# A two-layer encoder trunk with routed experts: the hot expert's extra part worked on fourth instead of seventh

## The reference

```python
def hierarchical_moe(h, w_rg, b_rg, w_re, b_re, w_gate, w_up, w_down):
    """Top-1 expert group, then top-2 SwiGLU experts inside that group."""
    ...
    for grp in range(MOE_GROUPS):
        hid = (jax.nn.silu(jnp.einsum('td,edf->tef', t, w_gate[grp]))
               * jnp.einsum('td,edf->tef', t, w_up[grp]))
        out = out + jnp.einsum('tef,efd->td', hid * gate[:, grp, :, None].astype(hid.dtype), w_down[grp])
    return out.reshape(b, s, d).astype(h.dtype)
```

## Time and profile before

| | us |
|---|---|
| median of 3 runs | 622.05 |
| lowest and highest | 620.03, 623.84 |
| profiled execution, its own time | 622.66 |
| its span in the trace | 620.9 |
| TensorE busy (matmul) | 545.1 (88%) |
| VectorE busy | 336.7 (54%) |
| ScalarE busy | 245.2 (39%) |
| GpSimd busy | 81.2 (13%) |

### The profile page before, as it was taken

The page is one execution under the profiler, slowest core; times in us unless marked ns, Lnnn a source line. Parts: engine busy times, 40 slices in busy tenths (PEclk is TensorE's granted clock), DMA queues, the critical chain, the costliest instruction groups (busy, mean ns, idle before and its releaser), DMA issues.

```text
span 620.9 us, 11990 instructions
## 1 busy us (share of the span) xinstructions
PE 545.1 (88%) x5109; PEld 451.7 (73%) x5109; DVE 336.7 (54%) x593; ACT 245.2 (39%) x457; POOL 81.2 (13%) x99
## 2 busy tenths in 40 slices
PE   2899986779979888884999999999999989788986
PEld 2899985679756466641999999899989856366642
DVE  2456759974562333447599655546646562433355
ACT  3453555254433133314545642443324533133221
POOL 6600242410100000001200290001110100000000
PEclk9999997969898999999899979999998898999999
DMA  8995400013989999999565252000021999999992
GB/s 310 276 344 167 170 2 1 1 68 125 398 341 413 410 406 409 409 410 374 170 204 186 66 194 69 2 3 4 2 69 66 407 335 392 409 409 409 409 409 112
DMA packets 55893, 145.24 MB, mean 234 GB/s; under 512 B 4260, under 2 KB 29040, under 8 KB 55712
## 3 DMA queue, kind: packets, MB, share of 16 engines
q1 hardware_dynamic: 54752, 142.47, 60.7%
q0 software_dynamic: 1088, 2.00, 1.5%
HBM read 143.40 MB, written 1.05 MB: 233 GB/s over the span
## 4 chain that ended last, share of the span: by engine, by line
PE 76%; DVE 13%; ACT 5%; issue 4%; DMA 2%; POOL 1%; SPq 0%; DVEq 0%; ACTq 0%
PE PS L1830 11%; PE PS L510 7%; PE PS L1791 7%; PE PS L511 7%; PE PS L512 6%; PE PS L1852 6%; PE PS L1866 3%; PE PS L546 3%; PE PS L547 3%; PE PS L548 3%; DVE WL L506 2%; PE PS L1867 2%; DVE X L1100 2%; PE PS L2126 2%; DMA RAW<-ev_w_in 2%
## 5 line engine op out<-in xcount | busy, mean ns | idle before, releaser
L506 DVE TENSOR_TENSOR WL<-RAW,WH 128x768 fp32r<-128x768 f32 (+2 forms) x96 | 82.8, 906 | 59.0 <-ACT WH L500 57.8
L510 PE MATMUL PS<-WH,HTH 128*128 128x384 f32 (+2 forms) x272 | 91.8, 338 | 3.1 <-DVE HTL L1100 1.4
L511 PE MATMUL PS<-WL,HTH 128*128 128x384 f32 (+2 forms) x272 | 90.3, 332 | 0.0
L512 PE MATMUL PS<-WH,HTL 128*128 128x384 f32 (+2 forms) x272 | 90.1, 331 | 0.0
L1100 DVE TENSOR_TENSOR X<-PS,X 128x512 f32<-128x512 f32 (+2 forms) x84 | 52.4, 662 | 62.6 <-PE PS L1867 49.0
L500 ACT ACTIVATE WH<-RAW 128x768 fp32r<-128x768 f32 (+2 forms) x96 | 70.7, 796 | 18.2 <-PE PS L512 10.4
L510 PEld LDWEIGHTS PS<-WH,HTH 128*128 128x128 f32 x272 | 53.1, 195 | 4.7 <-DVE HTL L1100 2.2
L511 PEld LDWEIGHTS PS<-WL,HTH 128*128 128x128 f32 x272 | 53.1, 195 | 0.0
L512 PEld LDWEIGHTS PS<-WH,HTL 128*128 128x128 f32 x272 | 52.8, 194 | 0.0
L546 PE MATMUL PS<-HTH,WH 128*128 128x256 f32 x160 | 46.6, 291 | 3.8 <-DVE HTL L1100 3.8
L547 PE MATMUL PS<-HTL,WH 128*128 128x256 f32 x160 | 46.1, 288 | 0.0
(11 more groups left out here) (344 smaller groups left out, 1051.1 us busy)
## 6 DMA issues: line engine op xcount, KB each, us to landing
RAW<-moe_w_gate SPq DMA_DIRECT2D x32, 512.0 KB, 11.3
RAW<-moe_w_up SPq DMA_DIRECT2D x32, 512.0 KB, 12.3
RAW<-moe_w_down SPq DMA_DIRECT2D x32, 512.0 KB, 13.9
XG<-moe_w_gate SPq DMA_DIRECT2D x32, 512.0 KB, 14.3
XG<-moe_w_up SPq DMA_DIRECT2D x32, 512.0 KB, 14.7
XD<-moe_w_down SPq DMA_DIRECT2D x32, 512.0 KB, 14.7
RAW<-od_w_in SPq DMA_DIRECT2D x9, 1536.0 KB, 8.2
RAW<-ev_w_in SPq DMA_DIRECT2D x6, 1536.0 KB, 12.9
```

Of the source, the lines that this page charges most:

```text
L506: done(nc.vector.tensor_tensor(out=lo, in0=raw, in1=hi.bitcast(F32), op=ALU.subtract), "unit_lo")
L510: nc.tensor.matmul(ps, ah, bh, start=start, stop=False)
L511: nc.tensor.matmul(ps, ah, bl, start=False, stop=False)
L512: return nc.tensor.matmul(ps, al, bh, start=False, stop=stop)
```

## The change

The extra part moves from place 6 (seventh) to place 3 (fourth). Its gather moves from the last place among those in the loop to the second, directly behind that of group 1; groups 2 and 3 are gathered behind places 3 and 5. Since the order of the gathers is no longer that of the group numbers, NTH gives the number of a group's gather in the order, and the semaphores' values are worked out from it. No instruction is added or removed. SP's program keeps its order; the values on which it waits follow from PLACE.

| place t | 0 | 1 | 2 | 3 | 4 | 5 | 6 | 7 | 8 |
|---|---|---|---|---|---|---|---|---|---|
| part before | 0 | 1 | 2 | 3 | 4 | 5 | extra | 6 | 7 |
| gather behind it, before | 1 | | 2 | 3 | extra | | | | |
| part after | 0 | 1 | 2 | extra | 3 | 4 | 5 | 6 | 7 |
| gather behind it, after | 1 | extra | | 2 | | 3 | | | |

```diff
-        ORDER = list(range(6)) + [QUADS, 6, 7]
+        ORDER = [0, 1, 2, QUADS, 3, 4, 5, 6, 7]
         PLACE = {q: t for t, q in enumerate(ORDER)}
...
-        GATHER_AFTER = {0: 1, 2: 2, 3: 3, 4: 4}
+        GATHER_AFTER = {0: 1, 1: G, 3: 2, 5: 3}
+        NTH = {g: n for n, g in enumerate([0] + list(GATHER_AFTER.values()))}
...
                 def gathered(g):
                     w = T if g < G else SPILL
                     for u in range(5):
-                        t = 5 * ((G + 1) * l + g) + u
+                        t = 5 * ((G + 1) * l + NTH[g]) + u
...
                 def silu(t):
                     q = ORDER[t]
                     act.wait_ge(sem("gu"), gate_ups(l, q))
-                    act.wait_ge(sem("m_gs"), (G + 1) * l + q // 2 + 1)
+                    act.wait_ge(sem("m_gs"), (G + 1) * l + NTH[q // 2] + 1)
...
                 def gate_slots(g):
-                    dve.wait_ge(sem("m_gg"), (G + 1) * l + g + 1)
+                    dve.wait_ge(sem("m_gg"), (G + 1) * l + NTH[g] + 1)
...
                 def gather(g):
...
-                        t = 5 * ((G + 1) * l + g) + u
+                        t = 5 * ((G + 1) * l + NTH[g]) + u
...
                 def gate_up(t):
-                    pe.wait_ge(sem("g_ev"), 5 * ((G + 1) * l + g) + 4)
+                    pe.wait_ge(sem("g_ev"), 5 * ((G + 1) * l + NTH[g]) + 4)
...
                 def combine(t):
-                    pe.wait_ge(sem("g_ev"), 5 * ((G + 1) * l + q // 2) + 5)
+                    pe.wait_ge(sem("g_ev"), 5 * ((G + 1) * l + NTH[q // 2]) + 5)
```

## The result

| | before | after |
|---|---|---|
| median of 16 runs each, us | 622.92 | 626.31 |
| lowest and highest | 620.03, 625.07 | 624.10, 633.32 |
| profiled execution, its own time (span) | 622.66 (620.9) | 626.29 (624.5) |

The ratio is 1.0065, with an interval of 1.0046 to 1.0084: 4.0 us slower than the 622.92 of before. The medians themselves lie 3.4 us apart, and the interval of the ratio is 2.9 to 5.2 us. The forecast was 2.9 us slower than the median then known (624.9), within the range of 620.5 to 628.5, and "within 1%" was the case with the highest chance.

The account below looks back on a forecast made before the run. Transfers were taken to bound quads 3 to 5, with early waits collecting at quad 7. Terms: 0 - 0.59 + 2 x 1.74 = +2.9 us, giving 624.9 us from the median of 622.05; range 620.5 to 628.5.

Parts of the forecast that it names:

- within 1%: Whole kernel: time differs from no change by less than 1% (6.2 us); chance 0.90.
- The bound: Quads 3 to 5, both layers: transfers are the bound, 15.34 us a quad at 410 GB/s; at quad 7 both arrive almost together.
- TensorE's steps: From quad 2 on: steps of 12.73, 9.19, 14.03, 9.24, 14.03, 9.24 us; ready for quad 7 at 271.89 in layer 0.
- The gain of 0.59 us in layer 1: Quad 7 of layer 1 starts at its landing, 604.04 instead of 604.63, behind a wait of 5.08 us.
- Layer 0: gain 0: Quad 7 of layer 0 still lands at 276.0; one wait of 4.23 us replaces four of the same sum.
- The hand-over: Quad 5's transfers, released only once quad 3 is multiplied: margin 5.1 us in layer 0, cost taken as 0.
- a queue that runs dry: Rival at the hand-over to quad 5: 2.5 us lost per layer, counted in full, giving 630.0 us; chance 0.06.
- The clock: Wait ahead of quad 7, both layers: TensorE's clock falls to half, slowing its products by 1.74 us each; both fall, chance 0.60.

Follow-up runs that it names:

- e5: Changed kernel with only 64 of 1024 columns of quad 3's down weights fetched in layer 1: 623.10 us, ratio 1.0001 to the kernel before.
- e6: Kernel before with only 64 of 1024 columns of quad 3's down weights fetched in layer 1: 619.64 us, ratio 0.9961.
- e12: Kernel before with the gain's reload issued behind quad 7's gate and up products of layer 0: 621.50 us, ratio 0.9989.
- e8: Changed kernel run again without further edits, beside the others: 626.87 us, ratio 1.0062 to the kernel before.
- e10: Kernel before with down weights of quads 3 and 4 of layer 1 cut to 64 of 1024 columns: 620.58 us, ratio 0.9958.
- e9: Changed kernel with down weights of quads 3 and 4 of layer 1 cut to 64 of 1024 columns: 622.31 us, ratio 1.0001.
- e7: Changed kernel with 4 (layer 0) and 5 (layer 1) unused products added in the wait ahead of quad 7: 623.25 us, ratio 1.0006.
- e2: Changed kernel with the gain's reload issued behind quad 7's gate and up products of layer 0: 624.90 us, ratio 1.0022 to the kernel before.
- e3: Changed kernel with the extra part fifth, between quads 3 and 4, its gather behind place 2: 625.08 us, ratio 1.0037 to the kernel before.

## Why the prediction was right, point by point

**The bound.** Right. The waits ahead of quads 3, 4 and 5 were for landings; they went, and came back at quad 7. e5 shows the end following the stream almost one to one in the changed kernel. The kernel before follows by about half: e6 gained 2.4 us of the 4.8 taken out, e12 some 0.7 of 1.2, which can't be told from none.

**TensorE's steps.** Right to about 0.2 us each. That it was ready for quad 7 at 272.02 against 271.89 is in part luck: quad 2 came 0.75 us later than in the profile before, and the steps add up to 0.62 less than in the working. In layer 1 quad 6 was to start without a wait; it waited 0.24 us, and 0.63 in e8.

**The gain of 0.59 us in layer 1.** Of the right size. From the issue of the extra part's weights to the start of quad 7 it is 97.2 us before (604.45 - 507.21), and 95.9 (606.11 - 510.25) and 96.2 in the two profiles of the changed kernel. In e12, with the old order, it is 96.4, so that the gain is somewhere from 0.2 to 1.3 us.

```profile
507.21 0.35 SPq L459 DMA_DIRECT2D SPW<-moe_w_gate  x1
```

```profile
510.25 0.35 SPq L460 DMA_DIRECT2D SPW<-moe_w_gate  x1
```

The wait there was 5.93 us, not 5.08, and the difference comes from TensorE's side. It reached quad 2 21.3 us behind the start of the stream (531.57 - 510.25), and 23.0 in the profile before (530.19 - 507.21), from which the forecast took it.

**Layer 0: gain 0.** Quad 7 started at 276.26 against 276.12. That it is so near hides two things: the stream had begun 0.73 us earlier than in the profile before, and took 0.9 us longer (96.7, not 95.8). Over all profiles the stream of layer 0 is 95.8, 95.8 and 97.3 us with the old order (the kernel before, e6, e10), 96.3 as their mean, and 97.2 as mean of the seven with the new one and the early reload. With the reload behind quad 7 the two orders agree, 95.5 (e12) and 95.8, so a loss, if there is one, comes with the reload's earlier moment. If these 0.9 us are real they are a small loss that I had put at 0. Three against seven executions don't settle it, and I did not test when in the stream the reload weighs most.

**The hand-over.** Right: there is a margin, no dip in the changed kernel, and a queue that runs dry in e9 with both cuts. For layer 1 the prediction has 1.3 us more of margin; by its own figures (563.1 - 555.9, less 5.1) it is 2.1, which changes nothing.

**The clock.** The mechanism is right, in both layers, and it accounts for all of the loss that can be told from noise: e7 with the wait filled is at 1.0006 (0.9981 to 1.0031). The ground given for it was weaker, that the new waits are longer than one followed by full clock: length alone does not decide, as the last section shows. The term was slightly undersized. In the five profiles with the long wait in layer 0 (the changed kernel, e2, e5, e8, e9) the products took 4.98, 6.24, 6.58, 6.53 and 4.93 us, 2.2 above 3.66 as a mean; in layer 1 (the changed kernel, e2, e8) 5.60, 5.28 and 5.16, 1.7 above. That is 3.9 us for both, where I took 2 x 1.74 = 3.5. With the 1.2 us that layer 1 gained in the same profiles, the sum by measured terms is 3.9 - 1.2 = 2.7, and with the open 0.9 of layer 0 it is 3.6; measured were 3.4 by the medians and 4.0 by the ratio. The forecast's two terms were both too small, 3.5 and 0.6 against 3.9 and 1.2, and this largely cancels in its 2.9.

Two profiles' spans, 3.6 us apart, say little by themselves: the stretch between the experts of layer 0 and the first quad of layer 1, which the change doesn't touch, took from 216.3 to 221.2 us in the 14 profiles.

## What to carry to other kernels

Before moving work into the gaps of an engine, ask what ends the last gap. If it is a stream of transfers, filling the early gaps only collects them into one ahead of the last piece, and one long wait of TensorE can cost more than several short ones of the same sum, as it did here, where its clock fell in or just behind it. A fall costs time only where no other wait follows that would have taken it up. Work that is moved ahead also holds its successors' buffers longer: check the time that the queue still has work for at the new moment of release.

## What I had not expected of the hardware

The length of a wait alone does not say whether the clock falls. Of the waits ahead of the gate and up products of the experts, it fell behind all nine of 3.98 to 5.93 us, but also behind waits of 2.33 us (e9), 2.40 (e7) and 2.59 (e5), all at quad 7, and did not behind 3.68 (e3, layer 0) or 3.07.

Nor does it have to fall while TensorE waits. Behind the short waits it came down only after the products had begun: quad 7 of e9 starts at 599.70, the clock is 1.00 up to 600 and 0.61 as mean of the next four us, with TensorE busy throughout.

```profile
596.00:600.00 4.00, 1.67 (x24) 0.43 (x20) 1.62 (x3) 1.19 (x2) 0.00 (x0) 1.00 1.02 409
600.00:604.00 4.00, 4.00 (x52) 2.60 (x48) 0.00 (x0) 0.00 (x0) 0.00 (x0) 0.61 0.76 301
```

And what it cost varied between 1.3 us and 2.9 for the same 64 products behind waits of nearly the same length (4.24 and 4.68 us in layer 0 of the changed kernel and of e5).
